# Mixture-of-experts router: experts chosen in two portions, logits right behind each row tile, low parts moved on VectorE

## What is computed

```python
x = x + hybrid_mixer(rms_norm(x, g1), ...)          # ends in  y @ w_out
t = rms_norm(x, g2)                                  # 512 x 1024
group_p = softmax(t @ w_router_group + b_router_group)       # 4 groups
gp, gi = top_k(group_p, 1)
exp_logits = (t @ w_router_expert + b_router_expert).reshape(n_tok, 4, 8)
sel = exp_logits of the chosen group
ev, ei = top_k(softmax(sel), 2); ev = ev / sum(ev); weights = gp * ev
for e in range(32):
    out += combine[:, e] * ((silu(t @ w_gate[e]) * (t @ w_up[e])) @ w_down[e])
```

## Time and profile before

| | us |
|---|---|
| median of 3 runs | 907.82 |
| lowest, highest | 902.79, 908.47 |
| the profiled execution, its own time | 912.77 |
| its span, first to last instruction | 911.0 |

### The profile page before, as it was taken

How to read it: one execution, slowest core, us unless ns; L and a number is a source line. 1 busy time by engine, 2 the same in 40 slices (tenths; PEclk the granted TensorE clock), 3 DMA queues, 4 the chain that set the end, 5 groups by cost and what they waited for, 6 DMA issues and landing times.

```text
span 911.0 us, 11270 instructions
## 1 busy us (share of the span) xinstructions
PE 800.3 (88%) x4126; PEld 615.0 (68%) x4126; DVE 565.3 (62%) x753; ACT 474.7 (52%) x660; POOL 269.3 (30%) x172
## 2 busy tenths in 40 slices
PE   4999985968689999999999983999999999999940
PEld 3788864867689788767874562677777777777730
DVE  4278989976733244320241236598888988888826
ACT  6224543355253333346211232588888888888823
POOL 2244415011420222337450002143534444342100
PEclk9999988988777899999999975899999999999975
DMA  8842222000000112224406146499999999899206
GB/s 238 277 139 93 92 93 93 0 1 1 1 1 2 37 57 75 110 93 177 153 20 281 47 157 253 140 353 371 372 379 352 374 352 367 346 347 366 95 16 272
DMA packets 49543, 159.26 MB, mean 175 GB/s; under 512 B 11176, under 2 KB 15288, under 8 KB 41182
## 3 DMA queue, kind: packets, MB, share of 16 engines
q1 hardware_dynamic: 42270, 150.28, 44.3%
q0 software_dynamic: 7232, 8.43, 2.8%
HBM read 152.38 MB, written 23.07 MB: 193 GB/s over the span
## 4 chain that ended last, share of the span: by engine, by line
PE 75%; DVE 11%; ACT 6%; issue 3%; DMA 2%; POOL 1%; SPq 1%; POOLq 0%; DVEq 0%; ACTq 0%
PE bank L397 18%; PE bank L399 17%; PE bank L398 17%; PE bank L741 6%; PE bank L786 3%; DVE arena L1562 3%; DVE bank L1544 2%; PE bank L515 2%; PE bank L644 1%; PE bank L569 1%; PE bank L536 1%; DVE arena L1970 1%; DVE arena L1560 1%; PE bank L546 1%; DMA arena<-in_w_in_dram 1%
## 5 line engine op out<-in xcount | busy, mean ns | idle before, releaser
L1796 DVE TENSOR_TENSOR gu_lo<-wgu,gu_hi 128x2048 fp32r<-128x2048 f32 x64 | 146.4, 2289 | 23.3 <-ACT gu_hi L1406 23.1
L1028 POOL TENSOR_TENSOR w_lo<-arena,w_hi 128x1024 fp32r<-128x1024 f32 x36 | 86.4, 2409 | 187.2 <-ACT w_hi L1151 187.2
L1406 ACT ACTIVATE gu_hi<-wgu 128x2048 fp32r<-128x2048 f32 x64 | 122.2, 1911 | 20.7 <-DMA wgu<-in_w_expert_up_dram 10.9
L397 PE MATMUL bank<-h_hi,w_hi 128*128 128x512 f32 x288 | 117.2, 407 | 4.2 <-DVE arena L1562 4.2
L398 PE MATMUL bank<-h_lo,w_hi 128*128 128x512 f32 x288 | 114.8, 399 | 0.0
L399 PE MATMUL bank<-h_hi,w_lo 128*128 128x512 f32 x288 | 114.8, 399 | 0.0
L1107 POOL DMA_INDIRECT arena<-h_rows,row_idx x32 | 80.4, 2512 | 106.7 <-DVE row_idx L1867 88.7
L397 PE MATMUL bank<-gu_hi,heT_hi 128*96 128x512 f32 x256 | 103.9, 406 | 2.5 <-DVE heT_lo L1891 1.9
L399 PE MATMUL bank<-gu_hi,heT_lo 128*96 128x512 f32 x256 | 102.2, 399 | 0.0
L398 PE MATMUL bank<-gu_lo,heT_hi 128*96 128x512 f32 x256 | 101.5, 397 | 0.0
L1113 POOL DMA_INDIRECT y_rows<-arena,row_idx x32 | 40.6, 1269 | 182.9 <-ACT arena L1445 182.9
(11 more groups left out here) (306 smaller groups left out, 1443.1 us busy)
## 6 DMA issues: line engine op xcount, KB each, us to landing
wgu<-in_w_expert_gate_dram SPq DMA_DIRECT2D x32, 1024.0 KB, 9.2
wgu<-in_w_expert_up_dram SPq DMA_DIRECT2D x32, 1024.0 KB, 19.0
wd<-in_w_expert_down_dram SPq DMA_DIRECT2D x32, 1024.0 KB, 14.1
arena<-in_w_in_dram SPq DMA_DIRECT2D x8, 2048.0 KB, 8.5
arena<-in_x_dram SPq DMA_DIRECT2D x8, 512.0 KB, 8.0
arena<-in_w_in_dram SPq DMA_DIRECT2D x4, 1024.0 KB, 10.6
y_rows<-arena SPq DMA_DIRECT2D x8, 512.0 KB, 10.2
arena<-in_w_out_dram SPq DMA_DIRECT2D x2, 2048.0 KB, 11.6
```

What stands on the lines that cost most here:

```text
L397: pe.matmul(o, wh, xh, start=first, stop=False)
L1028: gp.tensor_tensor(as_raw(w_lo[pslot(s)], s), raw(s), as_raw(w_hi[pslot(s)], s).bitcast(F32), ALU.subtract)\
L1406: act.activation(gu_hi[j % 2][:, :, ks, :], wgu[j][:, :, ks, :], ACT.Copy)\
L1796: TT(gu_lo[j][:, :, ks, :], wgu[j][:, :, ks, :], gu_hi[j % 2][:, :, ks, :].bitcast(F32), ALU.subtract)\
```

## The change

Four things are edited. TensorE: in the loop over the row tiles, `h2_tile(c-1)` comes behind the first half of tile c and `logits_tile(c-1)` behind the second; behind the loop there are the transposes and the logits of the last tile. The logits of the last tile go to a bank of their own, and each tile's logits have a mark of their own (`jobs[("logits", c)]`). VectorE: the choice of experts is a function `route(c0, c1)` of the row tiles, called for tiles 0 to 2 and then for tile 3. VectorE: the low parts of expert 0 move from ahead of the choice to behind the row list; the row list itself moves behind the overflow steps. Semaphore counts follow (`routed`, `route_dif`, `M_onehot`). ScalarE's order and SP's and GpSimd's programs stay as they are.

```diff
--- before.py
+++ after.py
@@ -717,9 +717,10 @@
                     end(ins, ("h2T", c, half), "route_mm")
 
             def logits_tile(c):
+                if c in (0, NT - 1):
+                    begin("logits", ("routed", 1 + c // (NT - 1)))
+                    held.append(jobs["logits"][0])
                 if c == 0:
-                    begin("logits", ("routed", 1))
-                    held.append(jobs["logits"][0])
                     wait(pe, "ld_part2", 64)
                     wait(pe, "rconst", 1)
                 b = bank[jobs["logits"][0]]
@@ -727,7 +728,7 @@
                 for k in range(KT):
                     ins = pe.matmul(b[:, c * NL:(c + 1) * NL], h2T[:, k, c * P:(c + 1) * P], wr_wide[k],
                                     start=(k == 0), stop=(k == KT - 1))
-                end(ins, "logits", "route_mm")
+                jobs[("logits", c)] = [jobs["logits"][0], "route_mm", tell(ins, "route_mm")]
 
             for c in range(NT):
                 for hf in range(NH2):
@@ -741,19 +742,14 @@
                         ins = pe.matmul(b[:], yT[:, m, c * P:(c + 1) * P], at(place[n], KT, HALF)[:, m, :], start=(m == 0),
                                         stop=(m == KT - 1))
                     end(ins, ("wo", c, hf), "wo_mm")
-                if c > 0:
-                    h2_tile(c - 1)
-                if c > 1:
-                    logits_tile(c - 2)
-
-
+                    if c > 0:
+                        (h2_tile, logits_tile)[hf](c - 1)
             h2_tile(NT - 1)
-            logits_tile(NT - 2)
             logits_tile(NT - 1)
             held.clear()
 
-            b = begin("rank", ("routed", 2))
-            wait(pe, "M_onehot", 1)
+            b = begin("rank", ("routed", 3))
+            wait(pe, "M_onehot", 2)
 
             hot = Mx.rearrange("p c n -> p (c n)")
             pe.matmul(b[:, 0:NT * NE], triu_s, hot, start=True, stop=False)
...
@@ -1796,39 +1792,46 @@
                 TT(gu_lo[j][:, :, ks, :], wgu[j][:, :, ks, :], gu_hi[j % 2][:, :, ks, :].bitcast(F32), ALU.subtract)\
                     .then_inc(S["w_glo"], 1)
 
-            gu_lo_half(0, 0, 0, 0)
-            gu_lo_half(0, 0, 0, 1)
-
             v.wait_ge(S["ld_rbias"], 32)
             v.wait_ge(S["rconst"], 6)
-            src = ready(v, "logits")
-            tell(TT(lg, src[:, 0:NT * NL].rearrange("p (c n) -> p c n", c=NT)[:, :, 0:NR], bc(rbias.unsqueeze(1), [P, NT, NR]),
-                    ALU.add), "routed")
-            v.wait_ge(S["routed"], 1)
-
-            def col(s, n):
-                return bc(sm[s].unsqueeze(2), [P, NT, n])
-
-            def first_max(dst, x, n, dsc, mx):
-
-                link(v.tensor_reduce(sm[mx], x, AX.X, ALU.max))
-                link(TT(dst, x, col(mx, n), ALU.is_equal))
-                link(TT(dst, dst, dsc, ALU.mult))
-                link(v.tensor_reduce(sm["ix"], dst, AX.X, ALU.max))
-                link(TT(dst, dst, col("ix", n), ALU.is_equal))
-
-            glog, elog = lg[:, :, 0:NG], lg[:, :, NG:NR]
-            first_max(ohg, glog, NG, descg, "gm")
-
-            TT(dg, glog, col("gm", NG), ALU.subtract).then_inc(S["route_dif"], 1)
-
-            link(TS(ohg, ohg, -NEG, NEG, ALU.mult, ALU.add))
-            link(TT(le.rearrange("p c (g e) -> p c g e", g=NG), elog.rearrange("p c (g e) -> p c g e", g=NG),
-                    bc(ohg.unsqueeze(3), [P, NT, NG, EG]), ALU.add))
-            first_max(oh1, le, NE, desc, "m1")
-            link(STT(out=rtmp, in0=oh1, scalar=4 * NEG, in1=le, op0=ALU.mult, op1=ALU.add))
-            first_max(oh2, rtmp, NE, desc, "m2")
-            TT(Mx, oh1, oh2, ALU.add).then_inc(S["M_onehot"], 1)
+
+            def route(c0, c1):
+
+                n = c1 - c0
+                cs = slice(c0, c1)
+
+                def col(s, w):
+                    return bc(sm[s][:, cs].unsqueeze(2), [P, n, w])
+
+                def first_max(dst, x, w, dsc, mx):
+
+                    link(v.tensor_reduce(sm[mx][:, cs], x, AX.X, ALU.max))
+                    link(TT(dst, x, col(mx, w), ALU.is_equal))
+                    link(TT(dst, dst, dsc[:, cs], ALU.mult))
+                    link(v.tensor_reduce(sm["ix"][:, cs], dst, AX.X, ALU.max))
+                    link(TT(dst, dst, col("ix", w), ALU.is_equal))
+
+                src = ready(v, ("logits", c1 - 1))
+                l = lg[:, cs, :]
+                done = tell(TT(l, src[:, c0 * NL:c1 * NL].rearrange("p (c n) -> p c n", c=n)[:, :, 0:NR],
+                               bc(rbias.unsqueeze(1), [P, n, NR]), ALU.add), "routed")
+                v.wait_ge(S["routed"], done)
+                glog, elog = l[:, :, 0:NG], l[:, :, NG:NR]
+                first_max(ohg[:, cs], glog, NG, descg, "gm")
+                TT(dg[:, cs], glog, col("gm", NG), ALU.subtract).then_inc(S["route_dif"], 1)
+                link(TS(ohg[:, cs], ohg[:, cs], -NEG, NEG, ALU.mult, ALU.add))
+                link(TT(le[:, cs].rearrange("p c (g e) -> p c g e", g=NG), elog.rearrange("p c (g e) -> p c g e", g=NG),
+                        bc(ohg[:, cs].unsqueeze(3), [P, n, NG, EG]), ALU.add))
+                first_max(oh1[:, cs], le[:, cs], NE, desc, "m1")
+                link(STT(out=rtmp[:, cs], in0=oh1[:, cs], scalar=4 * NEG, in1=le[:, cs], op0=ALU.mult, op1=ALU.add))
+                first_max(oh2[:, cs], rtmp[:, cs], NE, desc, "m2")
+                TT(Mx[:, cs], oh1[:, cs], oh2[:, cs], ALU.add).then_inc(S["M_onehot"], 1)
+
+            def col(s, w):
+                return bc(sm[s].unsqueeze(2), [P, NT, w])
+
+            route(0, NT - 1)
+            route(NT - 1, NT)
             for r, oh in enumerate((oh1, oh2)):
                 for q in range(2):
                     TT(codes[:, r, :, q, :], oh, bc(code_c[:, q, r, :].unsqueeze(2), [P, NT, NE]), ALU.mult)\
...
@@ -1860,11 +1863,6 @@
                         link(ins)
             TS(sm["v1"], sm["p1"], float(CAP), None, ALU.is_lt).then_inc(S["codes"], 1)
             TS(sm["v2"], sm["p2"], float(CAP), None, ALU.is_lt).then_inc(S["codes"], 1)
-            src = ready(v, "rows")
-            o = src[0:CAP, 0:2 * NE].rearrange("p (a b) -> p a b", a=2)
-            link(TS(ridx[0:CAP], o, 0.0, NO_ROW, ALU.is_equal, ALU.mult))
-            link(STT(out=ridx[0:CAP], in0=o, scalar=-1.0, in1=ridx[0:CAP], op0=ALU.add, op1=ALU.add))
-            v.tensor_copy(row_idx[0:CAP, :, :], ridx[0:CAP]).then_inc(S["idx_ready"], 1)
             link(v.tensor_copy(ovf[:, 1:2], ones[:, 0:1]))
             v.wait_ge(S["codes"], 6)
             for r, (oh, w) in enumerate(((oh1, "w1"), (oh2, "w2"))):
@@ -1881,6 +1879,13 @@
             link(TT(sm["mx"], sm["v1"], sm["v2"], ALU.add))
             link(TS(sm["mx"], sm["mx"], -1.0, 2.0, ALU.mult, ALU.add))
             v.tensor_reduce(ovf[:, 0:1], sm["mx"], AX.X, ALU.add).then_inc(S["route_dif"], 1)
+            src = ready(v, "rows")
+            o = src[0:CAP, 0:2 * NE].rearrange("p (a b) -> p a b", a=2)
+            link(TS(ridx[0:CAP], o, 0.0, NO_ROW, ALU.is_equal, ALU.mult))
+            link(STT(out=ridx[0:CAP], in0=o, scalar=-1.0, in1=ridx[0:CAP], op0=ALU.add, op1=ALU.add))
+            v.tensor_copy(row_idx[0:CAP, :, :], ridx[0:CAP]).then_inc(S["idx_ready"], 1)
+            gu_lo_half(0, 0, 0, 0)
+            gu_lo_half(0, 0, 0, 1)
             tell(v.tensor_copy(flag_i[0:1, 0:1], ready(v, "flag")[0:1, 0:1]), "flag_ready")
 
 
```

More of the change, by code:

```diff
@@ L764, in _ @@
             b = begin("rows", ("idx_ready", 1))
-            wait(pe, "M_onehot", 2)
+            wait(pe, "M_onehot", 3)
             for i in range(2 * NT):
@@ L771, in _ @@
             b = begin("flag", ("flag_ready", 1))
-            wait(pe, "route_dif", 3)
+            wait(pe, "route_dif", 4)
             ins = pe.matmul(b[0:1, 0:1], ones[:, 0:1], ovf[:, 0:1], start=True, stop=True)
@@ L1411, in _ @@
             gu_hi_half(0, 0, 0, 1)
-            act.wait_ge(S["route_dif"], 1)
+            act.wait_ge(S["route_dif"], 2)
             act.activation(dg, dg, ACT.Exp).then_inc(S["route_exp"], 1)
-            act.wait_ge(S["route_dif"], 2)
+            act.wait_ge(S["route_dif"], 3)
             act.activation(sm["tt"], sm["tt"], ACT.Exp).then_inc(S["route_exp"], 1)
@@ L1846, in _ @@
             tell(v.tensor_copy(pos.rearrange("p a b -> p (a b)"), src[:, 0:NT * NE]), "routed")
-            v.wait_ge(S["routed"], 2)
-            v.wait_ge(S["M_onehot"], 1)
+            v.wait_ge(S["routed"], 3)
+            v.wait_ge(S["M_onehot"], 2)
             v.wait_ge(S["codes"], 4)
```

## The result

The change made the kernel slower: 928.58 us (median of 6 runs, 925.50 to 929.66) against 907.15 us (6 runs, 902.79 to 912.17), ratio 1.0212, 95% interval 1.0185 to 1.0239. The ratio is not the quotient of the two medians (1.0236); the difference of the medians is 21.4 us, the interval of the ratio stands for 16.8 to 21.7 us. In a second series, on one chip, it was 927.96 against 910.05 us, ratio 1.0198 (1.0161 to 1.0235). Forecast were 920.9 us and a ratio of 1.015. The direction was right; the size was not, and the time lies outside the range of 912 to 926.

A forecast was written before the change was run, and what follows sets the result against it. The prediction took TensorE to bound the kernel, with the change acting only on the start of the expert loop. Its terms, 9.0 + 4.0 - 1.2 + 0.1 + 1.25 = +13.1 us on 907.8, gave 920.9 us, range 912 to 926.

The forecast's parts named there:

- What bounds the kernel: Whole kernel: TensorE is busy without a hole in the experts, so the change counts only through the start of their loop.
- The wait for the copies: Output projection: TensorE waits 3.2 us for ScalarE's copies behind the second halves of tiles 1, 2 and 3.
- The clock behind the waits: Output projection: TensorE's granted clock falls after each of two waits, 2.0 us each, +4.0 us.
- The end of the projection: Last projection matmul: +9.0 us from moved transposes, logits and two waits, and +4.0 us from the lower clock.
- The tail: From the last projection matmul to the one-hot sum `Mx`: 17.2 us instead of 18.44, -1.2 us.
- The row list: VectorE behind `Mx`: overflow steps of 2.9 us move into a wait of 2.8 us, +0.1 us.
- The gather: First gather on GpSimd: waits for the rest of the first low part, +1.25 us, bounds 0 and 3.4.
- The sum: Whole kernel: 9.0 + 4.0 - 1.2 + 0.1 + 1.25 = +13.1 us, median 920.9 us.
- The clock stays up: Rival, chance 0.14: TensorE's clock does not fall behind the projection's waits; +6.8 us, 914.6 us.
- No wait: Rival, chance 0.04: the logits of tile c-1 find ScalarE's copies made behind the second halves; 0.0 us, 907.8 us.
- The third rival: Chance 0.12: first gather waits for both low parts, +3.4 us, with clock losses of 2.4 each; +16.5 us, 924.3 us.

The follow-up runs named there:

- the kernel that copies first: Changed kernel with ScalarE copying the transposes of tile c-1 before it waits for the sums of tile c: 912.50 us, ratio 1.0025 to the kernel before.
- the filled kernel: Changed kernel with seven matmuls of unused product ahead of the logits of tiles 0, 1 and 2: 919.25 us, ratio 1.0099 to the kernel before.
- the kernel with all the filling: Kernel before with late low parts clear of the gather, ScalarE's first heT_hi earlier, four unused matmuls plus 30 more in TensorE's later waits: 907.83 us, ratio 0.9973.
- the kernel with the low parts alone: Kernel before with only the first expert's two low parts moved to right behind the row list: 910.46 us, ratio 1.0015.
- the kernel with both cures: Changed kernel with ScalarE copying before its square and root, row list ahead of overflow, and low parts spread around the gather: 910.45 us, ratio 0.9993.

## Why the prediction was right or wrong, point by point

- **What bounds the kernel.** Right. The expert loop moved as a block (80.00 of 80 us busy from 620 to 700 us before, and from 636 to 716 after), and the loss lies between the projection's first add and the first expert: 17.4 us, while the rest of the trace after is 1.5 us shorter.
- **The wait for the copies.** Right in place, number and size: 3.35, 3.26 and 3.26 us against 3.2. The wait was read out of the trace of before, where it did not exist, by laying two engines' orders beside each other.
- **The clock behind the waits: the term that was mis-sized.** It was put at 2.0 us for each wait, between 1.7 from a row of 3.9 us at half clock and 2.4 from a row of 5.2 us. The two waits cost 3.3 and 3.5 us. Against the same instructions at full clock (1.89 and 7.08 us in the kernel that copies first) the logits took 3.65 and 3.21 us, the half tile behind them 8.65 and 9.26: 1.76 + 1.32 + 1.57 + 2.18 = 6.8, beside 6.6 by the filled kernel. The step that failed is the length of the half-clock stretch: 6.0 and 6.5 us instead of 3.9 to 5.2, so the upper bound of 2.4 was too low as well. The trace of before held longer ones. It had 32 narrow matmuls in 6.93 us, all at half clock, without the clock coming back; the prediction read that it fell there "for good", but in the first expert it came back, after 5.4 us of nothing but wide matmuls at half:

```profile
568.50:574.00 5.50, 5.42 (x13) 3.62 (x14) 0.03 (x1) 0.74 (x1) 0.99 (x2) 0.50 0.27 85
```

  What sets the length is not shown. The longest two began with the logits' narrow matmuls, but wide ones alone also ran at half for over 5 us, here and behind the gap in the kernel with all the filling. Share of the miss: 3 us.
- **The end of the projection.** Forecast +9.0 and +4.0. Measured by the distance from the first add to the last: 548.01 - 480.16 = 67.85 against 532.61 - 481.08 = 51.53 us, +16.3: 6.6 the two waits, 2.6 the moved work, and the 7.1 left over is the clock (6.8 by its rows).
- **The tail.** Forecast -1.2, measured 564.42 - 547.98 = 16.4 against 18.4 us: -2.0. The logits of tile 2 took 2.65 us and not 3.46, since the clock fell in the middle of them (0.96 up to 552.5 us, 0.50 behind it). The choice for one tile took 564.42 - 560.06 = 4.4 us, as worked out; the one for three was covered. The prediction wrote off nothing for the store of `h2T_keep` and was right: ScalarE's high part behind it started 28.8 us behind the projection's last add, 29.4 before.
- **The row list.** Forecast +0.1; 574.26 - 564.42 = 9.8 us, as before (560.89 - 551.04).
- **The gather: the second mis-sized term, and the wrong end of its bounds.** Taken was 1.25 us, on the reasoning that the gather gets in behind the first low part. It waited for both: from 575.13 to 579.59, 0.9 us behind the end of the second. It landed 8.0 us behind the row list (582.25 - 574.26) instead of 4.9 (565.76 - 560.89): +3.1. The range had this end (3.4), the sum did not. The row used (2.88 us at 564.40) had one low part in front, and so could not tell "the rest of this instruction" from "until VectorE pauses". The rule cited from the Trainium skill (SBUF — State Buffer, Who interferes with whom), an exclusive lock for a whole instruction, gave the direction, and the trace agrees (4.46 us). That the waiting gather also stays out at the boundary of two long instructions is shown by the traces: it ended 0.9 us behind the second one here, in the kernel with the low parts alone, in the one that copies first and in the filled one. What let it in was small: between the second low part and a third one stood only the copy of the flag, 0.14 us at 578.58, and the gather ended at 579.59, in the middle of the third. Share of the miss: 1.9 us.
- **The sum.** 16.3 - 2.0 + 0 + 3.1 = 17.4 us by the traces against 13.1. With every term as measured the forecast would have been 907.8 + 17.4 = 925.2 us, inside the range of 912 to 926. The last 3.4 us up to 928.58 no trace explains; the interval of the ratio (16.8 to 21.7 us) does not tell them from nothing.
- **The rivals.** "The clock stays up" fell: it dropped at each of the two waits in the projection, in both traces. "No wait" fell in the kernel as changed, but it is what the kernel that copies first does: priced at 0.0, that kernel came out at +2.5 us by the medians, of which some 2 are the gather (its stretch is 89.0 us, that of the kernel with both cures 87.0), where the price had 1.25. The third rival, gather behind both low parts with a dearer clock (+16.5), had the right two mechanisms and was the nearest to what happened; it had got 0.12. Its argument was right too: the gather does wait when two low parts stand back to back, and a hand-over between the two did not let it in.

## What to carry to other kernels

Before work is moved ahead on one engine, read in which order the engine that feeds it does its own steps: a copy behind a square and a root was free as long as nobody asked for it early, and moving it two lines gave back 15.5 us. A pause of TensorE has two prices, the pause and the half clock behind it. The second was as dear as the first here (3.3 and 3.5 us for waits of 3.3), and is better bounded by the longest half-clock stretch of the trace than by the shortest. Two long VectorE instructions back to back right behind a list that an indirect DMA waited for delayed that DMA by both; one short instruction between such a pair and the next let it through.

## What had not been expected of the hardware

- Two low parts of 2.2 us back to back kept the first gather's record at 4.46 to 4.47 us in four kernels. With 2.9 us of short VectorE instructions first it was 1.06. A copy of 0.14 us between two low parts was enough to let it in.
- After a wait of 3.3 us the clock granted was 0.50 to 0.52 through 6.0 and 6.5 us of unbroken work that began with narrow matmuls; with the wait filled by matmuls of an unused product it was 1.00 over 39.9 us. In the first expert of the kernel before, wide matmuls alone ran at 0.50 for over 5 us.
- The same pause of 1.3 us left the clock at full in one trace of the kernel before (3.68 us for the logits) and halved it in the other (6.93 us).
